# Attention keys re-partitioned through a DRAM scratch tensor instead of by ScalarE copies

## The chip, the cores and the metric

The kernel runs on one core of one Trainium2 chip. The metric is device time in microseconds (us) of one execution. The median of three runs is 1271.83 us (1271.44 to 1271.86). The core's engines are named as in the profile: PE is TensorE (PEld its weight loads), DVE is VectorE, ACT is ScalarE, POOL is GpSimd and SP is SyncE, which issues transfers and computes nothing.

## The reference

Two decoder layers are computed for one sequence of 256 positions and a width of 2048. Each layer projects the residual stream `x` with one wide matrix, feeds three mixers side by side (dilated sliding-window attention, a spatial gating unit, a chunked mLSTM), multiplies each by a SiLU gate, projects the result back and applies `x = LayerNorm(alpha * x + out)`.

The change touches the attention alone. It has three groups of eight heads of 64 columns, with windows and dilations (128, 1), (512, 4) and (2048, 16). Cut to what matters:

```
aq, ak = apply_partial_rope(aq, cos, sin), apply_partial_rope(ak, cos, sin)
for gi, (window, dilation) in enumerate(ATT_GROUPS):
    q, k, v = the 8 heads of this group          # (256, 8, 64) each
    s = einsum('qc,kc->qk', q, k) * 64 ** -0.5   # per head, and per residue of the position mod dilation
    s = where(0 <= distance <= window // dilation, s, -inf)
    p = exp(s - max(s)); l = sum(p); o = (p @ v) / l; lse = max(s) + log(l)
att = sum over the groups of softmax(lse over groups) * o
```

Everything is float32.

## The kernel before

**Projections.** All weight columns pass as blocks of 512 columns, and a block as eight chunks of 256 rows (512 KB). SP loads a chunk into one of four buffers `w_raw` (L324) as soon as VectorE has finished with that buffer. ScalarE rounds it to `w_hi` (L736), VectorE subtracts to get the rest, `w_lo` (L1060), and TensorE runs 12 matmuls of 512 columns for the chunk (L373: high by high, high by low, low by high, for two row tiles of `x` and two halves of the chunk). `w_hi` and `w_lo` have four buffers each, so ScalarE and VectorE can be four chunks ahead of TensorE and no more. The order of work on every engine is written out by hand; each engine runs its list in order and stops at each semaphore until it has the value asked for.

**A group of the attention.** It has four blocks, in this order: queries (block `n0`), keys (`n0 + 1`), values (`n0 + 2`) and an mLSTM gate (`n0 + 3`). The three groups run in the order dilation 4, dilation 16, dilation 1. The first two are the compressed groups (`g < NCOMP`): positions are kept by their residue mod 4, and only keys of the same residue are scored. The third uses bands of 128 by 128.

The keys come out of the projection with positions on the partitions, and the scores want head columns on the partitions. The way there is:

- ScalarE and VectorE copy the block's two halves from PSUM into `z` (`take`).
- GpSimd applies the rotary turn (`rope(1)`), six instructions.
- VectorE transposes in 32 by 32 squares into `zT[1]`, a part of `arena` (`turn(1)`, L1133 for the third group, two instructions of L1137 for the others). In its list that stands after the split of the last chunk of block `n0 + 2` and before the first of block `n0 + 3`.
- The squares lie on the wrong partitions then. ScalarE moves them with 16 copies of 32 partitions by 256 numbers (`moved(1, ...)`, L807 for the compressed groups, L810 for the third) from `zT[1]` to `kT`, eight after the split of chunk 0 of block `n0 + 3` and eight after that of chunk 1. The last one counts up `qkT_act`.
- TensorE waits for that count and runs the scores: `comp_scores` (64 matmuls, L546) after chunk 1 of block `n0 + 3` in the compressed groups, `scores(0)` and `scores(1)` (L506, L507) after chunk 0 of it in the third. Then come chunks of the same block again, and between them, in the third group, the transposes of the probabilities (L518).

Queries go the same way during block `n0 + 2`, with 16 copies of their own.

SP's list holds the loads in the order of the chunks, and a few loads of gate rows:

```
sp.wait_ge(w_lo_done, (l * NBLK + n) * CH + (c + 1))
sp.dma_start(w_raw[:, c % RING], ...).then_inc(w_landed[c % RING], 16)
```

The lines that matter:

Of the kernel before, what the change touches and what calls it, by code (L numbers as in the profile page):

```python
# [21 lines left out]
P = 128  # L22
DEPTH, SEQ, D = 2, 256, 2048
# [13 lines left out]
NCOMP = 2  # L37
RES = 4
LEN = SEQ // RES
# [50 lines left out]
def hybrid_layers(nc, x, x_t, positions, w_in, gate_w, w_out, gate_bias, sgu_g, sgu_b, w_spatial, b_spatial,  # L90
                  conv_w, conv_b, head_g, ln_g, ln_b, ln_b_t, out):
    with ExitStack() as ctx:
# [20 lines left out]
        kT = arena[:, 1024:2048].rearrange("p (m t) -> p m t", m=PAIRS)  # L113
# [5 lines left out]
        qTr, kTr = (m.rearrange("p m (r i) -> p m r i", r=RES) for m in (qT, kT))  # L119
# [61 lines left out]
        stat_dram = nc.dram_tensor("stat_dram", (DEPTH, SEQ, 2 * HEADS), F32, kind="Internal").ap()  # L181
        gmax_dram = nc.dram_tensor("gmax_dram", (DEPTH, MH, SEQ), F32, kind="Internal").ap()
# [36 lines left out]
        qk_ps, qkT_act, qkT_dve = sem("qk_ps"), sem("qkT_act"), sem("qkT_dve")  # L219
# [79 lines left out]
        def _(sp):  # L299
            for l in range(DEPTH):  # L300
                def load(w, n, col, order, gate=()):

                    for c in range(CH):
# [15 lines left out]
                        if l == 0 and n == 0:  # L319
# [7 lines left out]
                                     ).then_inc(w_landed[c % RING], 16)  # L327

# [22 lines left out]
        def _(pe):  # L351
# [5 lines left out]
            for l in range(DEPTH):  # L357
# [134 lines left out]
                for g in range(GROUPS):  # L492
# [4 lines left out]
                    def scores(p):  # L497

                        if p == 0:
                            pe.wait_ge(qkT_act, qk + 2)  # L500
                            pe.wait_ge(comp_og_act, comp)
                            pe.wait_ge(comp_og_dve, comp)
                        for h in range(2):
                            rows = slice(HD * h, HD * (h + 1))
                            o = ps[4 + 2 * (p % 2) + h]
                            pe.matmul(o[:, 0:P], qT[rows, p, 0:P], kT[rows, p, 0:P], start=True, stop=True)  # L506
                            mm = pe.matmul(o[:, P:3 * P], qT[rows, p, P:2 * P], kT[rows, p, :],  # L507
# [30 lines left out]
                    def comp_scores():  # L538

                        pe.wait_ge(qkT_act, qk + 2)  # L540
# [182 lines left out]
        def _(act):  # L723
# [5 lines left out]
            for l in range(DEPTH):  # L729
# [55 lines left out]
                for g in range(GROUPS):  # L785
# [12 lines left out]
                    def moved(which, first, last):  # L798

                        act.wait_ge(turned, qk + which + 1)  # L800
                        for i in range(first, last):
                            u, f = i // 4, i % 4
                            src = zT[which][u * 32:(u + 1) * 32]
                            dst = (qT, kT)[which][f * 32:(f + 1) * 32]
# [7 lines left out]
                        if last == 16:  # L812
                            mv_.then_inc(qkT_act, 1)
# [56 lines left out]
                    for i in range(4):  # L870
                        split(n0 + 2, i, i + 1)
                        moved(0, 4 * i, 4 * i + 4)
# [900 lines left out]
```

## Time and profile before

| what | value |
|---|---|
| median of three runs | 1271.83 us |
| span of the profiled execution, first to last instruction | 1269.9 us |
| PE busy | 1257.0 us (99%) |
| PEld busy | 1040.2 us (82%) |
| DVE busy | 893.0 us (70%) |
| ACT busy | 705.4 us (56%) |
| POOL busy | 244.0 us (19%) |
| mean granted clock of TensorE | 0.997 |
| moved by DMA | 264.97 MB, 209 GB/s over the span |

The profiled execution's own time is its span of 1269.9 us; the median of the timed runs is 1.9 us above it. Busy time of PE is the union of matmuls that overlap, so it tells that there was always one under way, not at which pace; the pace is read from the chain of waits, where a stretch of matmuls stands with its length and count. A wait shows as idle time in front of an instruction, with the engine and line that ended it. The view of one line of DMA issues gives the time from the issue to the landing of the last byte.

### The profile page before, as it was taken

Reading aid. Unit: us, or ns where it says so; the run is one execution under the profiler, and the core shown is the slowest. Engines: PE = TensorE matmul, PEld = TensorE weight load, DVE = VectorE, ACT = ScalarE, POOL = GpSimd, SP = SyncE. Lnnn points to the kernel's source line nnn. Section 1 sums busy time; section 2 is a strip of 40 time slices with the busy share of each in tenths; the row PEclk is TensorE's granted clock in tenths of the full one; section 3 lists DMA queues with packets and bytes.
Section 4 is the critical chain, followed back from the end, with each engine's and each line's share of the span. In section 5 each row is a group of like instructions: output and inputs, shape, how many; then the busy total and the mean of one; then the engine's idle time right before and its main releaser. Section 6 shows DMA issues by size and latency. Waiting matters only on the chain.

```text
span 1269.9 us, 16388 instructions
## 1 busy us (share of the span) xinstructions
PE 1257.0 (99%) x6342; PEld 1040.2 (82%) x6342; DVE 893.0 (70%) x1229; ACT 705.4 (56%) x989; POOL 244.0 (19%) x268
## 2 busy tenths in 40 slices
PE   9999999999999999999999999999999999999996
PEld 8888888878888888888888788888888888888885
DVE  5686876876667655865785779768665776567656
ACT  5477476575555544444563775666755555345441
POOL 0321522522220000400003223334131200004000
PEclk9999999999999999999999999999999999999998
DMA  9968768765665555465657587678546556565562
GB/s 336 310 209 261 236 189 277 260 192 164 204 195 174 184 186 185 152 230 190 207 186 238 183 282 245 193 258 282 184 149 215 183 157 209 165 197 198 186 212 86
DMA packets 129277, 264.97 MB, mean 209 GB/s; under 512 B 8824, under 2 KB 8976, under 8 KB 128688
## 3 DMA queue, kind: packets, MB, share of 16 engines
q1 hardware_dynamic: 123712, 247.23, 60.6%
q0 software_dynamic: 3680, 13.28, 3.0%
q10 hardware_dynamic: 1808, 3.42, 0.7%
q8 instruction: 50, 0.82, 0.3%
q14 instruction: 27, 0.22, 0.0%
HBM read 258.61 MB, written 5.28 MB: 208 GB/s over the span
## 4 chain that ended last, share of the span: by engine, by line
PE 86%; ACT 4%; DVE 4%; POOL 3%; issue 2%; DVEq 0%; POOLq 0%; ACTq 0%
PE ps L373 79%; ACT arena L810 2%; DVE w_lo L1060 2%; ACT w_hi L736 2%; PE ps L444 1%; PE ps L671 1%; PE ps L391 1%; PE ps L639 1%; POOL arena L1684 1%; PE ps L533 0%; POOL arena L1680 0%; PE ps L518 0%; ACT arena L807 0%; PE ps L355 0%; DVE arena L1133 0%
## 5 line engine op out<-in xcount | busy, mean ns | idle before, releaser
L1060 DVE TENSOR_TENSOR w_lo<-w_raw,w_hi 128x1024 fp32r<-128x1024 f32 x408 | 527.1, 1305 | 326.4 <-ACT w_hi L736 324.5
L736 ACT ACTIVATE w_hi<-w_raw 128x1024 fp32r<-128x1024 f32 x408 | 427.3, 1058 | 388.9 <-PE ps L373 339.3
L373 PE MATMUL ps<-w_hi,xT_hi 128*128 128x512 f32 x1616 | 636.2, 394 | 0.7 <-DVE w_lo L1060 0.7
L373 PE MATMUL ps<-w_hi,xT_lo 128*128 128x512 f32 x1616 | 629.6, 390 | 0.0
L373 PE MATMUL ps<-w_lo,xT_hi 128*128 128x512 f32 x1616 | 629.0, 389 | 0.0
L373 PEld LDWEIGHTS ps<-w_hi,xT_hi 128*128 128x128 f32 x1616 | 303.4, 188 | 64.3 <-issue 1.3
L373 PEld LDWEIGHTS ps<-w_hi,xT_lo 128*128 128x128 f32 x1616 | 303.3, 188 | 64.0
L373 PEld LDWEIGHTS ps<-w_lo,xT_hi 128*128 128x128 f32 x1616 | 303.6, 188 | 61.4
L292 POOL TENSOR_TENSOR carried<-ident 1x1 f32<-1x1 f32 x30 | 19.6, 652 | 454.8 <-DVE arena L1416 178.7
L1217 DVE CUSTOM_DVE_ANT_0 mix<-xres,mix 128x1024 f32<-128x1024 f32 x64 | 89.0, 1390 | 1.1
L807 ACT ACTIVATE arena<-arena 32x256 f32<-32x256 f32 x128 | 53.2, 416 | 15.6 <-DVE arena L1137 14.0
L373 PE MATMUL ps<-ahead,xT_hi 128*128 128x512 f32 x160 | 49.8, 392 | 0.0
L1630 POOL TENSOR_TENSOR su<-z,sincos 128x128 f32<-128x128 f32 x24 | 23.6, 1005 | 122.0 <-ACT z L796 100.9
L1404 DVE SCALAR_TENSOR_TENSOR conv_y<-ps,cw,conv_y 128x255 f32<-128x255 f32 (+2 forms) x96 | 41.7, 476 | 1.1
L1060 DVE TENSOR_TENSOR ahead<-w_raw,ahead 128x1024 fp32r<-128x1024 f32 x23 | 27.5, 1223 | 15.1 <-ACT ahead L736 15.0
L736 ACT ACTIVATE ahead<-w_raw 128x1024 fp32r<-128x1024 f32 x23 | 23.8, 1056 | 22.8 <-DMA w_raw<-w_out_dram 7.2
L373 PEld LDWEIGHTS ps<-ahead,xT_hi 128*128 128x128 f32 x160 | 29.7, 188 | 5.9
L373 PE MATMUL ps<-ahead,xT_lo 128*128 128x512 f32 x80 | 31.2, 390 | 0.0
L810 ACT ACTIVATE arena<-arena 32x256 f32<-32x256 f32 x64 | 26.6, 416 | 7.3 <-DVE arena L1133 6.5
L825 ACT ACTIVATE arena<-arena 32x256 f32<-32x256 f32 x64 | 26.6, 415 | 6.8 <-DVE arena L1165 5.9
L967 ACT ACTIVATE arena<-conv_y 128x512 f32<-128x512 f32 x16 | 10.1, 633 | 32.7 <-DVE conv_y L1404 32.7
L1732 POOL TENSOR_TENSOR store<-store,hg 128x1024 f32<-128x1024 f32 x4 | 11.4, 2876 | 76.5 <-DVE store L1462 76.5
(244 smaller groups left out, 825.3 us busy)
## 6 DMA issues: line engine op xcount, KB each, us to landing
w_raw<-w_in_dram SPq DMA_DIRECT2D x367, 512.0 KB, 4.5
w_raw<-w_out_dram SPq DMA_DIRECT2D x64, 512.0 KB, 4.8
mix<-gate_w_dram SPq DMA_DIRECT2D x32, 512.0 KB, 5.6
xres<-x_dram ACTq DMA_DIRECT2D x4, 512.0 KB, 8.4
v_dram<-arena POOLq DMA_DIRECT2D x4, 512.0 KB, 6.3
z<-v_dram POOLq DMA_DIRECT2D x8, 256.0 KB, 5.6
z<-ln_g_dram POOLq DMA_DIRECT2D x2, 1024.0 KB, 7.7
store<-ln_b_dram POOLq DMA_DIRECT2D x2, 1024.0 KB, 7.9
```

Source lines behind the costliest of these rows:

```text
L292: nc.gpsimd.tensor_tensor(carried[0:1, at:at + 1], ident[0:1, 0:1], ident[0:1, 0:1], ALU.mult)
L373: mm = pe.matmul(ps[2 * s + t][:], a[:, order[c] * KC + k, t * P:(t + 1) * P], b[:, k], start=(c + k + i == 0), stop=(c == CH - 1 and k == ...
L391: tr = pe.transpose(ps[4 + u % 4][:, (k * TT + t) * P:(k * TT + t + 1) * P], src[:, t, at * P:(at + 1) * P], ident[:])
L444: mm = pe.matmul(ps[t][:], a[:, c * KC + k, t * P:(t + 1) * P], b[:, k], start=False, stop=(c == CH - 1 and k == KC - 1 and i == 2))
L736: A(hi_of(n, c), w_raw[:, c % RING], ACT.Copy).then_inc(w_hi_done, 1)
L807: mv_ = A(dst.rearrange("p m (r t u i) -> p u t (m r) i", r=RES, t=TT, u=4)[:, u], src.rearrange("p (t f q i) -> p f t q i", t=TT, f=4, i= ...
L810: mv_ = A(dst.rearrange("p m (t u s) -> p u t m s", t=TT, u=4)[:, u], src.rearrange("p (t m f s) -> p f t m s", t=TT, m=PAIRS, f=4)[:, f], ...
L825: e = A(pTC[f * 32:(f + 1) * 32, :, u * 32:(u + 1) * 32], zp[u * 32:(u + 1) * 32].rearrange("p (s f i) -> p f s i", s=SLOTS, f=4)[:, f], A ...
L1060: TTn(lo_of(n, c), w_raw[:, c % RING], hi_of(n, c).bitcast(F32), ALU.subtract).then_inc(w_lo_done, 1)
L1217: f = V.tensor_tensor_reduce(gate_junk, xres[:, tt, half * KH:(half + 1) * KH], gate_rows[buf], 1.0, 0.0, ALU.mult, ALU.add, gate_acc[:, t ...
L1404: f = STT(y, ps[4 + hf][:, t * SEQ:(t + 1) * SEQ - back], cw[:, m, j:j + 1], y, ALU.mult, ALU.add)
L1630: G.tensor_tensor(rope_a[:, :, :, c], v[:, :, :, c], trig(1), ALU.mult)
```

## The change

For the keys, the sixteen ScalarE copies of a group are replaced by transfers that SP issues. A DRAM tensor `k_dram` of 128 by 1024 numbers per layer and group is added. `put_keys` waits for VectorE's transposes and stores `zT[1]` there: two transfers of 256 KB in the compressed groups, one of 512 KB in the third, in runs of 512 bytes. `fetch_keys` waits until the store has landed and loads `kT` back with four transfers of 128 KB, each for 32 partitions, again in runs of 512 bytes. They stand in SP's list after the load of chunk 3 and after the load of chunk 4 of block `n0 + 3`. TensorE waits for the four landings (`kT_landed`) where it waited for the copies.

The keys have another order inside a partition: blocks of 128 numbers, each with 32 positions of the four head pairs. The score matmuls read them as runs of 8 numbers (compressed groups) or 32 numbers (third group) with 128 numbers from run to run; before, a run was contiguous. In the third group VectorE writes its transposes in the order that the store needs, in runs of 32 numbers. The queries' copies stay, and so does the place of everything else; the splits of chunks 0 to 2 of block `n0 + 3` now follow one another on ScalarE.

```diff
+        kTr = kT.rearrange("p (b m r i) -> p m r b i", b=SEQ // QUARTER, m=PAIRS, r=RES)
+        kTt = kT.rearrange("p (b m s) -> p m b s", b=SEQ // QUARTER, m=PAIRS)
...
+        k_dram = nc.dram_tensor("k_dram", (DEPTH, GROUPS, 4, TT, 4, QUARTER, P), F32, kind="Internal").ap()
...
+                def put_keys(g):
+                    sp.wait_ge(turned, l * (GROUPS * 2) + g * 2 + 2)
+                    dst = k_dram[l, g].rearrange("f t u j x -> t (u j) f x")
+                    src = zT[1].rearrange("p (t f x) -> p t f x", t=TT, f=4)
+                    if g < NCOMP:
+                        for t in range(TT):
+                            sp.dma_start(dst[t], src[:, t]).then_inc(kT_put, 16)
+                    else:
+                        dst = k_dram[l, g].rearrange("f t u j x -> (u j) (f t) x")
+                        sp.dma_start(dst, zT[1].rearrange("p (a x) -> p a x", a=4 * TT)).then_inc(kT_put, 32)
+                def fetch_keys(g):
+                    sp.wait_ge(kT_put, (l * GROUPS + g + 1) * 32)
+                    src = k_dram[l, g].rearrange("f t u j x -> f j (t u) x")
+                    dst = kT.rearrange("p (b x) -> p b x", b=SEQ // QUARTER)
+                    for f in range(4):
+                        sp.dma_start(dst[f * QUARTER:(f + 1) * QUARTER], src[f]).then_inc(kT_landed, 16)
...
+                        if N_LOOP < n < N_SU and (n - N_LOOP) % 4 == 3:
+                            if c == 3:
+                                put_keys((n - N_LOOP) // 4)
+                            if c == 4:
+                                fetch_keys((n - N_LOOP) // 4)
...
-                            pe.wait_ge(qkT_act, qk + 2)
+                            pe.wait_ge(qT_act, l * GROUPS + g + 1)
+                            pe.wait_ge(kT_landed, (l * GROUPS + g + 1) * 4 * 16)
...
-                            pe.matmul(o[:, 0:P], qT[rows, p, 0:P], kT[rows, p, 0:P], start=True, stop=True)
-                            mm = pe.matmul(o[:, P:3 * P], qT[rows, p, P:2 * P], kT[rows, p, :],
+                            pe.matmul(o[:, 0:P], qT[rows, p, 0:P], kTt[rows, p, 0:P // QUARTER], start=True, stop=True)
+                            mm = pe.matmul(o[:, P:3 * P], qT[rows, p, P:2 * P], kTt[rows, p],
...
-                                                   kTr[rows, p, r, :], start=True, stop=True)
+                                                   kTr[rows, p, r], start=True, stop=True)
...
-                    split(n0 + 3, 0, 1)
-                    moved(1, 0, 8)
-                    split(n0 + 3, 1, 2)
-                    moved(1, 8, 16)
-                    split(n0 + 3, 2, 3)
+                    split(n0 + 3, 0, 3)
...
-                            V.transpose(zT[which], z[:, which].rearrange("p t c -> p (t c)")).then_inc(turned, 1)
+                            into = zT[which].rearrange("p (f b s) -> p b f s", f=4, b=TT * PAIRS) if which else zT[which]
+                            V.transpose(into, z[:, which].rearrange("p t c -> p (t c)")).then_inc(turned, 1)
```

## Rows read from the trace of the kernel before

**Rows 1.** The page, busy us of each engine (share of the span), count.

```profile
PE 1257.0 (99%) x6342; PEld 1040.2 (82%) x6342; DVE 893.0 (70%) x1229; ACT 705.4 (56%) x989; POOL 244.0 (19%) x268
```

**Rows 2.** The chain of waits in order of time: start us, us, what.

```profile
99.22 1.09 PE ps L546 x64
100.31 24.71 PE ps L373 x108
...
728.41 1.09 PE ps L546 x64
```

**Rows 3.** Waits of PE: line, waited for, us in total, times, longest.

```profile
PE ps L373 <- DVE w_lo L1060: 0.7, 1, 0.7
```

**Rows 4.** Timeline of PE, third groups: start us, us, instructions, [idle before <- releaser].

```profile
276.32 0.50 PE L506 MATMUL ps<-arena 64*128 64x128 f32 x4 [0.46 <-ACT arena L810]
...
905.01 0.50 PE L506 MATMUL ps<-arena 64*128 64x128 f32 x4
```

**Rows 5.** View of line L518: idle before it, us, times.

```profile
  ACT arena L839: 1.0, 2
```

**Rows 6.** The page, copy groups: count | busy us, mean ns | idle before.

```profile
L807 ACT ACTIVATE arena<-arena 32x256 f32<-32x256 f32 x128 | 53.2, 416 | 15.6 <-DVE arena L1137 14.0
...
L810 ACT ACTIVATE arena<-arena 32x256 f32<-32x256 f32 x64 | 26.6, 416 | 7.3 <-DVE arena L1133 6.5
```

**Rows 7.** Timeline of ACT, third group, layer 0: the last eight copies.

```profile
272.87 3.40 ACT L810 ACTIVATE arena<-arena 32x256 f32<-32x256 f32 x8
```

**Rows 8.** Timeline of DVE, the keys' transposes of four of the six groups.

```profile
86.53 2.09 DVE L1137 STREAM_TRANSPOSE arena<-z 128x512 f32<-128x512 f32 x2
...
267.10 1.23 DVE L1133 STREAM_TRANSPOSE arena<-z 128x1024 f32<-128x1024 f32 x1
...
716.90 2.09 DVE L1137 STREAM_TRANSPOSE arena<-z 128x512 f32<-128x512 f32 x2
...
895.78 1.23 DVE L1133 STREAM_TRANSPOSE arena<-z 128x1024 f32<-128x1024 f32 x1
```

**Rows 9.** View of line L324, five windows: issue ns, start; then issue to landing.

```profile
L324 SPq DMA_DIRECT2D w_raw<-w_in_dram x1: 367/367/367, 267.2 to 267.2; - x1
DMA to landing us min/median/max: 5.2/5.2/5.2
...
L324 SPq DMA_DIRECT2D w_raw<-w_in_dram x1: 368/368/368, 269.5 to 269.5; - x1
DMA to landing us min/median/max: 4.7/4.7/4.7
...
L324 SPq DMA_DIRECT2D w_raw<-w_in_dram x1: 368/368/368, 274.1 to 274.1; - x1
DMA to landing us min/median/max: 3.4/3.4/3.4
...
L324 SPq DMA_DIRECT2D w_raw<-w_in_dram x1: 368/368/368, 717.0 to 717.0; - x1
DMA to landing us min/median/max: 4.9/4.9/4.9
...
L324 SPq DMA_DIRECT2D w_raw<-w_in_dram x1: 368/368/368, 895.9 to 895.9; - x1
DMA to landing us min/median/max: 4.8/4.8/4.8
```

**Rows 10.** DMA issues by line: count, KB each, median us from issue to landing.

```profile
z<-v_dram POOLq DMA_DIRECT2D x8, 256.0 KB, 5.6
...
out_dram<-xres SPq DMA_DIRECT2D x4, 512.0 KB, 2.7
arena<-o_dram POOLq DMA_DIRECT2D x2, 512.0 KB, 4.6
```

**Rows 11.** Busy us by window: PE, PEld, DVE, ACT, POOL, granted clock, DMA.

```profile
1259.90:1262.70 2.80, 0.00 (x0) 0.00 (x0) 2.70 (x6) 0.29 (x1) 0.00 (x0) 1.00 0.00 0
1263.00:1269.90 6.90, 0.00 (x0) 0.00 (x0) 3.73 (x4) 0.00 (x0) 0.00 (x0) 0.50 0.38 152
```

More of the change, by code:

```diff
@@ L38 @@
 RES = 4
+QUARTER = P // 4
 LEN = SEQ // RES
@@ L112, in hybrid_layers @@
         qT = arena[:, 0:1024].rearrange("p (m t) -> p m t", m=PAIRS)
-        kT = arena[:, 1024:2048].rearrange("p (m t) -> p m t", m=PAIRS)
+        kT = arena[:, 1024:2048]
         vA = arena[:, 2048:3072].rearrange("p (t c) -> p t c", t=TT)
@@ L118, in hybrid_layers @@
         oacc = arena[:, 6400:7424].rearrange("p (t c) -> p t c", t=TT)
-        qTr, kTr = (m.rearrange("p m (r i) -> p m r i", r=RES) for m in (qT, kT))
+        qTr = qT.rearrange("p m (r i) -> p m r i", r=RES)
+        kTr = kT.rearrange("p (b m r i) -> p m r b i", b=SEQ // QUARTER, m=PAIRS, r=RES)
+        kTt = kT.rearrange("p (b m s) -> p m b s", b=SEQ // QUARTER, m=PAIRS)
         vS = vA.rearrange("p t (h q d) -> p t q h d", h=2, q=PAIRS)
@@ L218, in hybrid_layers @@
         mask_set, roped, turned = sem("mask_set"), sem("roped"), sem("turned")
-        qk_ps, qkT_act, qkT_dve = sem("qk_ps"), sem("qkT_act"), sem("qkT_dve")
+        qT_act, kT_put, kT_landed = sem("qT_act"), sem("kT_put"), sem("kT_landed")
         scored, masked, probs = sem("scored"), sem("masked"), sem("probs")
@@ L538, in comp_scores @@
                     def comp_scores():
-                        pe.wait_ge(qkT_act, qk + 2)
+                        pe.wait_ge(qT_act, l * GROUPS + g + 1)
+                        pe.wait_ge(kT_landed, (l * GROUPS + g + 1) * 4 * 16)
                         for j in range(TT):
@@ L796, in take, with moved @@
                         A(dst, src, ACT.Copy).then_inc(z_act, 1)
-                    def moved(which, first, last):
-                        act.wait_ge(turned, qk + which + 1)
+                    def moved(first, last):
+                        act.wait_ge(turned, qk + 1)
                         for i in range(first, last):
                             u, f = i // 4, i % 4
-                            src = zT[which][u * 32:(u + 1) * 32]
-                            dst = (qT, kT)[which][f * 32:(f + 1) * 32]
+                            src = zT[0][u * 32:(u + 1) * 32]
+                            dst = qT[f * 32:(f + 1) * 32]
                             if g < NCOMP:
@@ L812, in moved @@
                         if last == 16:
-                            mv_.then_inc(qkT_act, 1)
+                            mv_.then_inc(qT_act, 1)
                     def comp_exponentials():
@@ L871, in _ @@
                         split(n0 + 2, i, i + 1)
-                        moved(0, 4 * i, 4 * i + 4)
+                        moved(4 * i, 4 * i + 4)
                     take(n0 + 2, 0, z[:, 1, 0, :])
                     split(n0 + 2, 4, 8)
-                    split(n0 + 3, 0, 1)
-                    moved(1, 0, 8)
-                    split(n0 + 3, 1, 2)
-                    moved(1, 8, 16)
-                    split(n0 + 3, 2, 3)
+                    split(n0 + 3, 0, 3)
                     if g < NCOMP:
```

## The prediction

> **What bounds the kernel now.** The first view to read is the page's list of busy times. TensorE (PE) is busy for 1257.0 of the 1269.9 us of the span [rows 1]; ScalarE (ACT), from which the copies go, is busy for 56% of it. The second is the chain of waits, in order of time: long pieces of it are the projection matmuls and nothing else, and one shows their pace: 108 matmuls, nine weight chunks of 12, in 24.71 us, so 2.75 us a chunk [rows 2]. The third is what TensorE waited for. The view of its waits has one delay of a matmul by VectorE (DVE) over the whole program, 0.7 us [rows 3]; the score matmuls of the third group wait 0.46 us for ACT's key copies in layer 0 and for nothing that the row shows in layer 1 [rows 4]; the transposes of the probabilities have 1.0 us of idle weight loading before them, for the exponentials [rows 5]. Together that is 2.2 us; the first of them is in the query part of a group, which the change leaves alone. What the change can give back is therefore at most 0.5 + 1.0 us, while a key matrix that comes late stops TensorE at once, since its instructions run in order.
>
> **What is removed.** Half of the 128 copies of L807 and half of the 64 of L810, 416 ns each [rows 6]: 96 copies, 40 us of ACT time over the program, 6.7 us a group. None of that is on TensorE's path by itself. In the stretch before the scores of the third group, layer 0, the last eight copies run from 272.87 to 276.27 [rows 7], and the two weight splits that were put between them came in time for TensorE. So the 40 us are worth nothing but the waits named above: 0.5 us for the scores of layer 0, and some of the 1.0 us before the probabilities, because ACT and VectorE reach them with no backlog of splits. Of that last one I take 0.4 (between 0 and 1.0; part of an idle weight load lies beside matmuls still draining). The query copies stay, and VectorE's order of work stays.
>
> **What is added, and where it waits.** The keys' way after VectorE's transposes is now: SyncE (SP) sees the semaphore, one or two transfers of 512 KB in all to DRAM, their landing, four transfers of 128 KB back, their landing, the scores. The distance that this has to fit in is from the end of the transposes to the start of the scores. For the third group: 267.10 + 1.23 = 268.33 to 276.32, and 895.78 + 1.23 = 897.01 to 905.01 [rows 4, 8], so 8.0 us in both layers, of which 7.5 in layer 0 before TensorE is idle. For the other two groups, whose scores come one chunk later: 86.53 + 2.09 = 88.62 to 99.22 is 10.6 us [rows 2, 8], two more groups show the same within 0.1, and layer 1's first has only 718.99 to 728.41, 9.4 us [rows 2, 8].
>
> *The store.* It enters SP's queue right behind weight loads that are still in flight. In layer 0's third group the load issued at 267.2 lands after 5.2 us, at 272.4, and the next one in the queue, issued at 269.5, lands after 4.7, at 274.2, which is 1.8 us later [rows 9]. The store is issued at 268.4 and takes that place, so I let it land 1.8 us after the load in front of it. Its rows are 512 bytes long, and no row shows such a store; the bounds are 0 and 1.0 us more: a 512 KB load of 2 KB rows from POOL takes 4.6 us where half as much in 1 KB rows takes 5.6 [rows 10]. I take 0.4, nearer to the load in the same queue. The store lands at 274.6. An alone store of 512 KB takes 2.7 us [rows 10], which is the low end: 271.1.
>
> *The fetch.* SP is woken, and issues four transfers at 0.37 us each. A load with nothing in front of it takes 3.4 us [rows 9]; that is the low end, counted from the first issue. Counted from the last it is 3.4 + 1.1 = 4.5, and behind another load 4.7 [rows 9]. The data of the first three moves while the fourth is issued, so I take 3.4 + 0.7, and again 0.4 for the short rows: 4.5 us.
>
> *Sum by group.* Layer 0, third: 274.6 + 4.5 = 279.1 against 276.32, so 2.8 us later. Layer 1, third: the load issued at 895.9 lands after 4.8, at 900.7 [rows 9]; plus 1.8, 0.4 and 4.5 is 907.4 against 905.01, 2.4 us later. Layer 1, first: the load at 717.0 lands after 4.9, at 721.9 [rows 9]; plus 6.7 is 728.6 against 728.41, 0.2 us. The other three have 1.2 us more room than that one and stay hidden with about 1 us to spare. Together 2.8 + 2.4 + 0.2 - 0.4 = **5.0 us slower**. So 0.9 us of waits go, and larger ones stand in the same places.
>
> *Edits that I cost at nothing.* SP's wait for the store holds the loads of chunks 5 to 7 of that block behind it: chunk 5 was issued at 274.1 in layer 0 [rows 9] and now goes after the fetch's issues, at about 276. It lands some 4 us after that, while TensorE needs it four chunks of 2.75 us after the scores; without that cover every us of SP's wait over 5 would be lost. The transfers add 1 MB a group to the queues, as much as two weight chunks of the 32; their queueing is already in the 1.8 us, and the loads behind them have the same four chunks of room. In the third group VectorE writes its transposed keys in runs of 32 instead of in one piece: between 1.23 us (contiguous) and 2.09 us (the two strided ones of the other groups) [rows 8]. The store waits for the loads in front of it for longer than that, so it costs nothing. The score matmuls read keys in runs of 8 or 32 numbers that are 512 bytes apart; no row shows a moving operand like that. Between 0 and a doubling of 1.09 us [rows 2] in four groups, I take 0, the value of the row that stands for as many matmuls of as many columns.
>
> **The rivals.**
>
> 1. *The transfers run as if alone and the keys are in time* (not slower). Store 2.7 and fetch 3.4 make 6.1 us after the transposes: 274.4 and 903.1, before TensorE comes to the scores. It decides from 7.5 us of both together. For it: the store is SBUF to DRAM, and one such is the fastest large transfer of the profile. Against: loads are in flight at the moment of issue in each of the six groups. Gain 0.5 + 0.4, so 1270.9. The Trainium skill, page DMA: Bandwidth & Descriptors, section Anatomy of one DMA — SWDGE (gpsimd) path, gives a transfer about 2.0 us plus its bytes over 436 GB/s; by that an estimate is 3.2 us for 512 KB and 6.4 for the two, and the sum would end here. The trace agrees for a load alone (3.4 us) and not for loads behind others (4.7 to 5.2) [rows 9].
>
> 2. *TensorE's clock falls in the new wait.* After the last matmul the granted clock is still 1.00 over 2.8 us without TensorE work, and 0.50 in the stretch from 1263 on [rows 11]. My wait in layer 0 is 279.1 - 275.9 = 3.2 us. If the clock falls to 1.2 GHz, each chunk until it rises costs 2.75 us more; one or two chunks make 2.7 to 5.5, and with one of the two waits over the edge the time is about 1281. Against: the waits are at the edge of what that row shows, and the matmuls around them are dense. The Trainium skill, page TensorE: Matmul & The Clock Gate, section HAM oscillation — how this bites in real kernels, says that waits for transfers can send the array back to half rate so that the next work starts slow; rows 11 show the fall, and no row of this case shows the price.
>
> 3. *Short rows and four small transfers cost 1 us more in each direction.* Then the third groups lose 4.8 and 4.4, layer 1's first 2.2, and each of the other three 1.0: 14.4 - 0.4 = 14.0, so 1286. For it: the 1 KB rows of rows 10. Against: those are POOL's.
>
> 4. *The scores read the spread keys at half speed*: 4.4 us more, 1281.
>
> **How the numbers follow.** The profiled execution lasts 1269.9 us from first to last instruction, 1.9 below the median of 1271.83, and 5.0 us are added to both: 1274.9 and **1276.8 us**. What a measurement of this kernel can tell from no change is about 0.2%, 2.5 us. Chances: the forecast 0.52, its own range 1273.5 to 1279.5; rival 1 0.15; rival 2 0.16; rival 3 0.13; rival 4 0.04. No case reaches a gain of 2.5 us, since the three waits together are 2.2: faster 0.02, for what the trace does not show. Same takes rival 1 and the low tenth of the forecast, 0.23; the rest is slower, 0.75. The range is from rival 1, 1271, to rival 3, 1286, which leaves out the far side of rivals 2 and 3.
>
> **What would show it.** Right: a TensorE gap of 2 to 4 us before the scores of the third group in both layers, released by the fetch; none or under 1 us in the other groups; a store that lands about 6 us after the transposes, a fetch 4 to 5 us after its first issue; ACT about 40 us less busy at an unchanged pace of 2.75 us a chunk. Wrong: scores of the third group that start within 0.5 us of where they did; gaps of several us in all six groups; a granted clock under 1.00 behind a gap; or a pace that changes away from the scores, which would say that ACT's copies cost TensorE something that no wait shows.

## The result and the profile after

The changed kernel takes 1280.13 us, the median of four runs (1276.17 to 1280.63), where the kernel before takes 1271.82 beside it: a ratio of 1.006, with a 95% interval of 1.0045 to 1.0074. That is 8.3 us slower, 3.3 more than the sum of the prediction. The profiled execution took 1279.92 us, with a span of 1278.2.

The page's busy times of the changed kernel, to be read against [rows 1]:

```profile
PE 1258.5 (98%) x6342; PEld 1041.7 (81%) x6342; DVE 895.8 (70%) x1229; ACT 667.9 (52%) x893; POOL 242.5 (19%) x268
```

ScalarE is relieved of 96 instructions and 37.5 us; TensorE runs the same 6342 matmuls in 1.5 us more. The rest of the loss is idle time of TensorE. The view of PE's waits in the changed kernel (line, waited for: us in total, times, longest), against [rows 3]:

```profile
PE ps L536 <- issue: 5.8, 2, 3.4
PE ps L577 <- DMA arena<-k_dram: 1.6, 1, 1.6
PE ps L384 <- POOL ident L1595: 1.6, 1, 1.6
PE ps L402 <- DVE w_lo L1087: 0.7, 1, 0.7
```

The first two rows are new, and both stand in front of score matmuls: L536 in the third groups, L577 in a compressed one. The last two stand in the view of before as well, with the same 1.6 and 0.7 us. "Issue" names no releaser, but the timeline of PE gives the moment, and the queue's own timeline shows what landed then. PE's timeline of the changed kernel, three places, against [rows 4] and the second chain row of [rows 2]:

```profile
279.55 0.50 PE L536 MATMUL ps<-arena 64*128 64x128 f32 x4 [3.38 <-issue]
...
734.52 1.16 PE L577 MATMUL ps<-arena 64*64 64x64 f32 x64 [1.61 <-DMA arena<-k_dram]
...
913.62 0.50 PE L536 MATMUL ps<-arena 64*128 64x128 f32 x4 [2.38 <-issue]
```

SyncE's timeline of the changed kernel, the third group of layer 0, layer 1's first group and layer 1's third (L312 and L315 are the store, L323 the fetch, L348 weight loads):

```profile
267.36 0.37 SPq L348 DMA_DIRECT2D w_raw<-w_in_dram  x1
268.51 0.44 SPq L315 DMA_DIRECT2D k_dram<-arena  x1
269.62 0.38 SPq L348 DMA_DIRECT2D w_raw<-w_in_dram  x1
274.85 1.81 SPq L323 DMA_DIRECT2D arena<-k_dram  x4
...
723.56 0.92 SPq L312 DMA_DIRECT2D k_dram<-arena  x2
...
728.34 1.82 SPq L323 DMA_DIRECT2D arena<-k_dram  x4
...
903.23 0.39 SPq L315 DMA_DIRECT2D k_dram<-arena  x1
...
909.17 1.81 SPq L323 DMA_DIRECT2D arena<-k_dram  x4
```

The fetch's first issue is the moment at which SyncE saw the store landed. So the store took 6.3 us in layer 0's third group (268.51 to 274.85) and 5.9 in layer 1's, and the last of the four fetches landed 4.6 and 4.4 us after the first issue, 0.1 us ahead of the scores. Keys that were done at 268.5 are usable at 279.5.

The starts of the same 6342 matmuls in the two traces give where the 8.3 us came in (us, later than before):

| place | change |
|---|---|
| the first 10 us of the program | +0.27 |
| third group's scores, layer 0 | +2.92 |
| the matmuls behind them, at half clock | +1.46 |
| probabilities' transposes, layer 0 | -0.23 |
| first group's scores, layer 1 | +1.69 |
| third group's scores, layer 1 | +2.43 |
| probabilities' transposes, layer 1 | -0.21 |
| sum | 8.3 |

The first line is not the change's: in the traces of the other kernels below, the same matmuls come between 0.3 us earlier and 0.7 us later than before. The third line is read from the busy times by window, whose last three figures are the granted clock, the DMA engines' share and GB/s:

```profile
275.70:279.60 3.90, 0.52 (x5) 0.13 (x3) 0.60 (x1) 1.06 (x1) 0.00 (x0) 1.00 0.89 235
280.40:283.80 3.40, 3.40 (x15) 2.36 (x13) 3.21 (x21) 1.79 (x8) 0.00 (x0) 0.50 0.69 259
283.80:290.00 6.20, 6.20 (x32) 5.15 (x31) 2.46 (x3) 3.72 (x12) 0.00 (x0) 1.00 0.40 108
```

After 3.4 us without a matmul the granted clock is still 1.00 when the scores start at 279.55; it is 0.50 from 280.4 to 283.8, and full again after. The DMA engines are 89% busy during the wait: weight loads and key transfers at once.

The line in the table for layer 1's first group has a cause of its own. Its fetch took 6.0 us, from 728.34 to 734.38; the chain of waits of the changed kernel shows the last of its four pieces, which took 4.7, where the median of all 24 is 2.6:

```profile
729.69 4.69 DMA arena<-k_dram
```

What ran beside it is GpSimd's store of the group's values, 512 KB. Its row in GpSimd's timeline of the changed kernel, then of the one before:

```profile
728.80 0.78 POOL L1677 DMA_DIRECT2D v_dram<-arena  x1 [0.28 <-issue]
```

```profile
730.99 0.78 POOL L1649 DMA_DIRECT2D v_dram<-arena  x1
```

TensorE's matmuls stand 4.4 us later there than before (the first four lines of the table), so against them the values' store came 6.6 us earlier: 0.5 us behind the fetch's first issue, where before it came behind the scores. The timelines of ScalarE and VectorE show why. ScalarE's half of the values, which the store waits for, stood behind two times eight key copies; VectorE's half, taken at 729.18, stood behind a split that waited 3.28 us for ScalarE, which these copies held up. Both halves are now taken at 727.50. ScalarE and VectorE before, then ScalarE in the changed kernel:

```profile
723.53 3.40 ACT L807 ACTIVATE arena<-arena 32x256 f32<-32x256 f32 x8
726.95 1.06 ACT L736 ACTIVATE w_hi<-w_raw 128x1024 fp32r<-128x1024 f32 x1
727.91 0.58 ACT L796 ACTIVATE arena<-ps 128x512 f32<-128x512 f32 x1
```

```profile
728.04 1.22 DVE L1060 TENSOR_TENSOR w_lo<-w_raw,w_hi 128x1024 fp32r<-128x1024 f32 x1 [3.28 <-ACT w_hi L736]
```

```profile
727.50 0.60 ACT L827 ACTIVATE arena<-ps 128x512 f32<-128x512 f32 x1 [1.31 <-PE ps L402]
```

### The profile page after: what moved, and what is told of

Same layout as the page of the kernel before. It is cut to its first block, busy times and chain, and to the rows that moved or that the text cites. A ratio compares the mean times of both kernels' runs of the same rounds, so it can differ in the third digit from the quotient of the medians.

```text
span 1278.2 us, 16332 instructions
## 1 busy us (share of the span) xinstructions
PE 1258.5 (98%) x6342; PEld 1041.7 (81%) x6342; DVE 895.8 (70%) x1229; ACT 667.9 (52%) x893; POOL 242.5 (19%) x268
## 4 chain that ended last, share of the span: by engine, by line
PE 95%; DVE 1%; issue 1%; ACT 1%; DMA 1%; SPq 0%; DVEq 0%; POOL 0%; POOLq 0%; ACTq 0%
PE ps L402 88%; PE ps L473 1%; PE ps L702 1%; PE ps L420 1%; PE ps L670 1%; DVE w_lo L1087 1%; PE ps L563 0%; ACT arena L838 0%; PE ps L548 0%; PE ps L384 0%; DMA arena<-k_dram 0%; PE ps L577 0%; PE ps L596 0%; DMA k_dram<-arena 0%; ACT w_hi L767 0%
## 5 line engine op out<-in xcount | busy, mean ns | idle before, releaser
L296 POOL TENSOR_TENSOR carried<-ident 1x1 f32<-1x1 f32 x30 | 13.7, 458 | 435.4 <-DVE arena L1444 178.7
L856 ACT ACTIVATE arena<-arena 32x256 f32<-32x256 f32 x64 | 26.6, 415 | 6.8 <-DVE arena L1193 6.0
L838 ACT ACTIVATE arena<-arena 32x256 f32<-32x256 f32 x64 | 26.6, 416 | 5.5 <-DVE arena L1165 4.6
```

The costliest lines, as they stand in the source:

```text
L296: nc.gpsimd.tensor_tensor(carried[0:1, at:at + 1], ident[0:1, 0:1], ident[0:1, 0:1], ALU.mult)
L838: mv_ = A(dst.rearrange("p m (r t u i) -> p u t (m r) i", r=RES, t=TT, u=4)[:, u], src.rearrange("p (t f q i) -> p f t q i", t=TT, f=4, i= ...
L856: e = A(pTC[f * 32:(f + 1) * 32, :, u * 32:(u + 1) * 32], zp[u * 32:(u + 1) * 32].rearrange("p (s f i) -> p f s i", s=SLOTS, f=4)[:, f], A ...
```

## The experiments

Theory T: the loss is the scores' wait for the keys' way through DRAM; that way is long because weight loads, and in one group the store of the values, run on the same DMA engines (or meet in the DRAM behind them, which no run here tells apart); and the clock falls behind the longest wait. Rivals: A, the transfers slow the rest of the kernel, whoever waits for them. B, the form of the transfers (512-byte runs, four pieces) makes them slow. C, the store is late only because of its place in SyncE's queue. All ratios are to the kernel before on the same chip, with 95% intervals.

**1. Nobody waits for the keys.** All transfers run, but the fetch goes to a tile that nobody reads, and the scores read zeros, so the attention's values are not the reference's. Later steps that write over the store's source wait for the store instead (not shown).

```
+        kT_aside = sb("kT_aside", [P, 1024])
-                    dst = kT.rearrange("p (b x) -> p b x", b=SEQ // QUARTER)
+                    dst = kT_aside[:].rearrange("p (b x) -> p b x", b=SEQ // QUARTER)
-                            pe.wait_ge(kT_landed, (l * GROUPS + g + 1) * 4 * 16)
+                G.memset(kT, 0.0)
```

> All transfers run, at the places they have in the changed kernel, but the fetch lands in a tile of its own and the scores read zeros in place of the keys (left out: the scores' use of the keys); so no matmul waits for a transfer. Theory (the time is lost where the scores wait for the fetch, and by the clock behind such a wait): the three waits of 2.9, 1.7 and 2.4 us and the 1.5 us at half clock go, so about 8.5 us off the changed kernel: 1271 to 1272, no granted clock under 1.00 after the first 10 us. Rival A (the added traffic, SP held at the store, or the reads of keys in short runs cost it): 1276 or more, with gaps or a slower pace elsewhere.

1270.84 us, ratio 0.9992 (0.9983 to 1.0001). PE's waits in it:

```profile
PE ps L388 <- POOL ident L1602: 1.6, 1, 1.6
PE ps L406 <- DVE w_lo L1092: 0.7, 1, 0.7
PE ps L461 <- ACT ahead L797: 0.4, 1, 0.4
```

No score waits, the granted clock stays up, and the whole loss is gone. The transfers themselves cost nothing that can be measured: A is out. The medians are 0.9 us under the kernel before, with an interval that reaches no change; the starts of the same matmuls show where such a gain sits, 0.5 us at the third group's scores in layer 0 and 0.2 us at the probabilities' transposes of each layer. So ScalarE's 96 copies were worth about 0.9 us, and no arrangement that was tried gives more.

**2. The third group's keys by ScalarE again**, the compressed groups' as changed.

```
-                        if N_LOOP < n < N_SU and (n - N_LOOP) % 4 == 3:
+                        if N_LOOP < n < N_LOOP + NCOMP * 4 and (n - N_LOOP) % 4 == 3:
+                        moved_keys(0, 8)
                         split(n0 + 3, 1, 2)
+                        moved_keys(8, 16)
```

> The compressed groups' keys go by transfers, the third group's by ScalarE copies in the old order. Theory: the losses of the third groups go (2.9 + 2.4 us and 1.5 us at half clock), the 0.4 us before the probabilities come back, and the 1.7 us of layer 1's first group stay: 1273 to 1274. Rival A (traffic and short runs, spread evenly over six groups): two thirds of the 8.3 us stay, about 1277. Rival B (the wait in layer 1's first group is an accident of one execution): 1271.5 to 1272.5.

1272.78 us, ratio 1.0009 (1.0000 to 1.0018), a little under the forecast. The row of its PE waits for the keys:

```profile
PE ps L579 <- DMA arena<-k_dram: 0.7, 1, 0.7
```

Layer 1's first group still waits, and the third groups lose next to nothing: their scores start 0.15 us sooner in layer 0 and 0.25 us later in layer 1 than before. So 7.3 of the 8.3 us hang on the third groups' transfers and on what they bring (less of a wait in layer 1's first group is among it: 0.8 us there instead of 1.7; why that one shrank was not tried by itself).

**3. TensorE kept at work in the wait**: ten matmuls of the identity ahead of the third group's wait, into a bank that is free there.

```
+                            for _ in range(10):
+                                pe.matmul(ps[7][:, 0:P], ident[:], ident[:], start=True, stop=True)
                             pe.wait_ge(qT_act, l * GROUPS + g + 1)
                             pe.wait_ge(kT_landed, (l * GROUPS + g + 1) * 4 * 16)
```

> Ten matmuls of the identity by itself, which nobody reads, stand before TensorE's wait for the third group's keys; they take about 2.3 us of it. Theory (the clock fell because TensorE was idle): the granted clock stays 1.00 behind layer 0's third group, and 1.5 us go where the clock fell: 1276 to 1278.7, with the scores no later than they were. Rival C (the clock falls for another reason, or the fill delays the scores): 1280 or more.

1277.57 us, ratio 1.0046 (1.0032 to 1.0059): 2.6 us less than the changed kernel. PE's timeline around the wait, and the busy times of the window there:

```profile
276.42 2.39 PE L532 MATMUL ps<-ident 128*128 128x128 f32 x20
279.07 0.50 PE L538 MATMUL ps<-arena 64*128 64x128 f32 x4 [0.26 <-DMA arena<-k_dram]
```

```profile
278.30:281.00 2.70, 2.44 (x23) 1.87 (x21) 0.96 (x8) 0.00 (x0) 0.00 (x0) 1.00 0.99 362
```

The scores still come late, by 2.0 us in layer 0 and 2.7 in layer 1, but the clock stays at 1.00, there and in the 5 us behind it, and its mean is 0.997 or 0.998 in all five runs. With something to wait on, the view names the releaser too: the fetch. So the fall of the clock belongs to a TensorE that stands idle and is paid on top of the wait, 1.46 us in the profiled execution of the changed kernel. The rest of the 2.6 us is not the clock's: the wait in layer 0 was itself 0.9 us shorter (the store took 5.8 us, not 6.3), and layer 1's first group lost 1.1 us, not 1.7; why was not tried. The changed kernel's four timed runs spread over 4.5 us, and the shortest is the one with the highest mean clock (0.997, the others 0.994 to 0.996), which fits a fall that comes in some runs and not in others; but the kernel of this experiment spreads over 2.7 us too, so the fall is not all of it.

**4. The store ahead of one load**: in all six groups, the store goes in front of the load of chunk 3 and not behind it.

```
+                        if N_LOOP < n < N_SU and (n - N_LOOP) % 4 == 3 and c == 3:
+                            put_keys((n - N_LOOP) // 4)
                         sp.wait_ge(w_lo_done, (l * NBLK + n) * CH + (c + 1))
...
-                            if c == 3:
-                                put_keys((n - N_LOOP) // 4)
```

> The store stands in SP's list ahead of the load of chunk 3 and no longer behind it, so one load less is in front of it in the queue. Theory (the store's 6.3 us in the third group are mostly the loads in front): it lands about 1.6 us earlier in the third groups and 1 to 1.5 in the others, the scores follow, and the clock does not fall: 1273.5 to 1276. Rival D (a store to DRAM of 512-byte runs takes its 5 to 6 us whatever stands in front): within 1 us of the changed kernel, 1279 to 1281.

1282.62 us, ratio 1.0081 (1.0067 to 1.0095): a miss, slower even than the changed kernel. SyncE's timeline, third group of layer 0:

```profile
271.00 0.44 SPq L315 DMA_DIRECT2D k_dram<-arena  x1
271.48 1.50 SPq L350 DMA_DIRECT2D w_raw<-w_in_dram  x2
275.32 1.81 SPq L323 DMA_DIRECT2D arena<-k_dram  x4
```

The store did get quicker, 4.3 us instead of 6.3. But the two loads issued right behind it were now in front of the fetch, which took 6.6 us instead of 4.6 (the last one landed at 281.94): 10.9 us in both kernels from the store's issue to the keys. What one leg gains the other gives back, as long as the loads go between them. What makes this kernel slower than the changed one is the compressed groups, of which three wait for the keys here and one there:

```profile
PE ps L577 <- DMA arena<-k_dram: 3.1, 3, 1.6
```

**5. The values' store waits for the keys**:

```
                         carry_pool()
+                        pool.wait_ge(kT_landed, (l * GROUPS + g + 1) * 4 * 16)
                         pool.dma_start(v_dram[l, g].rearrange("(t p) c -> p t c", p=P), vA).then_inc(v_stored, 16)
```

> GpSimd's store of the values (512 KB), which in the changed kernel comes during the keys' fetch because ScalarE is done with its list earlier, waits for the keys' landing. Theory (in layer 1's first group the fetch took 6.0 us instead of 4.7 because that store ran beside it): the fetch takes 4.5 to 4.8 us in all compressed groups and the wait of 1.7 us there falls under 0.5; the third groups are as in the changed kernel; 1.2 to 1.5 us less in the sum of the waits. Rival F (the fetch varies by itself): a wait of 1 us or more in some compressed group.

1275.90 us, ratio 1.0040 (1.0028 to 1.0052), 4.2 us less than the changed kernel. The one row that PE's waits have left for scores:

```profile
PE ps L536 <- issue: 4.6, 2, 3.0
```

The row of L577 is gone, and the fetch of that group takes 4.8 us instead of 6.0 (727.45 to 732.27): the collision with the values' store is shown. It is not the scatter of one trace: numbers 9 to 12 below hold that store back too and lose at most 0.1 us there, while numbers 2, 3 and 6, whose compressed groups are the changed kernel's, lose 0.8, 1.1 and 1.2. The third groups, which have no such store, still wait. The medians differ by more than the 1.7 us of this group: in the profiled execution (1277.16 us) the third groups lose 2.5 and 1.7 us, 0.4 and 0.7 less than in the changed kernel, and the clock falls as it does there; why they lose less was not tried.

**6. Another form of transfer** in the third group: four stores with runs of 1 KB, one fetch with runs of 4 KB.

```
+                        for u in range(4):
+                            sp.dma_start(k3_dram[l, :, :, u, :].rearrange("f j x -> j f x"), src[u * QUARTER:(u + 1) * QUARTER]).then_inc(kT_put, 16)
...
+                        sp.dma_start(kT, k3_dram[l].rearrange("f j u x -> (f j) (u x)")).then_inc(kT_landed, 64)
```

> Third group only: the store goes as four transfers of 128 KB in runs of 1 KB, the fetch as one of 512 KB in runs of 4 KB. Theory (the loads in the queue set when the store lands; the fetch is 3.4 us of a lone load and 1.3 us of three further issues): the store lands where it did within 0.5 us, the fetch takes 3.4 to 3.8 us instead of 4.6, the waits of the third groups are 1 us shorter and the clock does not fall: about 1276.5. Rival G (the fetch waits for the load in front of it whatever its form): fetch 4.4 us or more, 1278 to 1281.

1277.55 us, ratio 1.0043 (1.0027 to 1.0058), its profiled execution 1280.66. SyncE's timeline, layer 0:

```profile
268.00 1.99 SPq L317 DMA_DIRECT2D k_dram<-arena  x4
...
273.40 0.42 SPq L323 DMA_DIRECT2D arena<-k_dram  x1
273.86 11.37 SPq L353 DMA_DIRECT2D w_raw<-w_in_dram  x4
```

One fetch with runs eight times as long took 5.7 us (273.40 to 279.06), longer than the four short ones, probably because the next loads were issued 0.5 us behind it and not 1.9; that was not tried by itself. The third groups lost 3.1 and 2.8 us, and the clock was at 0.50 for 6.8 us of the profiled execution, which cost another 2.8. So another form does not help beside the loads; that the short runs cost little in themselves is shown by numbers 11 and 12, where a store in 512-byte runs takes 3.2 us with no load near, against 2.7 for the large store of [rows 10]. B is out as the cause.

**7. Store and fetch ahead of the loads of chunks 3 and 4, in all six groups.**

```
+                        if N_LOOP < n < N_SU and (n - N_LOOP) % 4 == 3 and c == 3:
+                            put_keys((n - N_LOOP) // 4)
+                            fetch_keys((n - N_LOOP) // 4)
+                        weights(c)
```

> Store and fetch both stand ahead of the loads of chunks 3 and 4, so neither has a fresh load in front of it. Theory (each 512 KB load that stands in the queue before the store or between store and fetch costs the keys about 2 us, wherever it stands): store 4.2 us, fetch 4.0 to 4.6, the keys land 8.2 to 8.8 us after the transposes instead of 11.0; waits of at most 1 us in the third groups and none in the others, no fall of the clock: 1271.3 to 1273. Rival E (chunks 3 and 4 are then late for TensorE): gaps of 1 to 3 us in front of the projection matmuls two or three chunks after the scores, 1274 or more.

1274.53 us, ratio 1.0022 (1.0014 to 1.0031). SyncE's timeline in the third group of layer 0, then the first row of PE's waits:

```profile
267.98 0.44 SPq L315 DMA_DIRECT2D k_dram<-arena  x1
271.83 1.81 SPq L323 DMA_DIRECT2D arena<-k_dram  x4
273.69 2.81 SPq L331 DMA_DIRECT2D w_raw<-w_in_dram  x4
```

```profile
PE ps L404 <- DVE w_lo L1089: 2.6, 2, 1.9
```

With no load between the two legs, the keys are there 8.0 us after the store's issue, no score waits, and the clock stays up. The price moved: in layer 1's first group four loads come in a bunch from 724.33 on, behind the fetch and beside the values' store, take 5.2 to 9.7 us, and a projection chunk waits 1.9 us for its weights.

**8. Another queue**: ScalarE issues the store and the fetch, SyncE only loads.

```
+                    split(n0 + 3, 0, 1)
+                    put_keys(g)
+                    split(n0 + 3, 1, 2)
+                    fetch_keys(g)
+                    split(n0 + 3, 2, 3)
```

> Store and fetch are issued by ScalarE, on its own queue, and SP's list has only the loads. Theory (it is the order in SP's queue): the transfers pass the loads, store 3.5 us and fetch 4.0 to 4.6 us, keys 7.5 to 8.5 us after the transposes, waits of the third groups under 1 us: 1271.3 to 1273. Rival H (the 16 engines are shared, and the transfers lose as much to the loads beside them as they lost behind them): keys still 10 us or more after the transposes, 1277 or more. Rival I (ScalarE, held at the store's landing, is late with its splits): gaps in front of the projection matmuls.

1282.76 us, ratio 1.0088 (1.0075 to 1.0101). ScalarE's timeline, third group of layer 0:

```profile
268.25 0.64 ACTq L746 DMA_DIRECT2D k_dram<-arena  x1
...
275.51 1.85 ACTq L754 DMA_DIRECT2D arena<-k_dram  x4
```

On a queue with no load in it the store took 7.3 us, longer than anywhere: C is out. SyncE, which no longer waited for it, put one more load beside it. The scores waited 3.5 and 2.8 us, and the clock fell behind both waits. The Trainium skill, page DMA: Bandwidth & Descriptors, section Issuing engines are not separate DMA queues, says that transfers from any issuing engine run on the same 16 DMA engines and interleave; these 7.3 us agree.

**9 and 10. The best parts together**: in the third group store and fetch ahead of the loads of chunks 3 and 4, the compressed groups as changed, the values' store behind the keys. Number 9 also has the third group's transposes one weight split earlier.

```
+                        if n == N_SU - 1 and c == 3:
+                            put_keys(NCOMP)
+                            fetch_keys(NCOMP)
...
+                        pool.wait_ge(kT_landed, (l * GROUPS + g + 1) * 4 * 16)
... number 9 only:
-                    split(n0 + 2, 6, 8)
+                    split(n0 + 2, 6, 7 if g == NCOMP else 8)
                     turn(1)
+                    if g == NCOMP:
+                        split(n0 + 2, 7, 8)
```

> Third group: store and fetch ahead of the loads of chunks 3 and 4, and VectorE's key transposes before its split of chunk 7 of the values' block instead of behind it (1.2 us earlier); compressed groups as in the changed kernel, with GpSimd's store of the values behind the keys' landing. Theory: keys land 8 us after the transposes and 1 us before the scores in the third groups, no wait there, and none over 0.4 us in the compressed groups, no fall of the clock: 1270.8 to 1271.8, at or under the kernel before by up to 1 us. Rival E (the loads of chunks 3 and 4 of the third group come late for TensorE or for the exponentials): gaps there of 0.5 us or more, 1272 to 1274.

> The same without the earlier transposes. Theory: the third groups' scores come within 0.3 us of the kernel before, as they did with both transfers ahead of the loads in all groups, and the late chunks of layer 1's first group (2.4 us there) are gone: 1271.3 to 1272.5, 0.5 to 1 us above the one with earlier transposes. Rival: 1273.5 or more, if the lateness came from holding the loads in the third group too.

Number 10: 1272.16 us, ratio 1.0004 (0.9995 to 1.0014), as expected. Number 9: 1273.62, ratio 1.0015 (1.0007 to 1.0024), a miss: earlier keys made it slower. SyncE's timeline of number 9, then of number 10, third group of layer 0:

```profile
265.11 1.76 SPq L351 DMA_DIRECT2D w_raw<-w_in_dram  x2
267.66 0.44 SPq L315 DMA_DIRECT2D k_dram<-arena  x1
273.40 1.95 SPq L323 DMA_DIRECT2D arena<-k_dram  x4
```

```profile
264.60 1.76 SPq L351 DMA_DIRECT2D w_raw<-w_in_dram  x2
268.29 0.44 SPq L315 DMA_DIRECT2D k_dram<-arena  x1
272.14 1.81 SPq L323 DMA_DIRECT2D arena<-k_dram  x4
```

The store of number 9 was issued 0.6 us earlier and landed 1.3 us later. The second of the two loads in the first row went out at 266.51 there, 1.15 us ahead of the store; in number 10 at 266.00, 2.29 us ahead.

**11 and 12. Is it the distance to the load in front?** Numbers 10 and 9 again, with the load of chunk 2 behind the fetch as well.

```
-                        if n == N_SU - 1 and c == 3:
+                        if n == N_SU - 1 and c == 2:
```

> As the kernel that sends the third group's store and fetch ahead of the loads of chunks 3 and 4 (and holds the values' store back until the keys have landed), but with the load of chunk 2 behind them too, so that the nearest load in front of the store was issued some 3.6 us before it, not 2.3. Theory (what counts is how far the load in front is from being done when the store is issued: 1.15 us after its issue the store took 5.5 to 6.4 us, 2.29 us after it 3.7 to 4.3): the store now takes 2.7 to 3.5 us, the fetch about 4.2, the keys are there 7 to 7.8 us after the transposes, no score waits, 1271.0 to 1272.2 us. Rival (the store has its own fixed time of about 3.8 us here, from its 512-byte rows): store 3.8, keys at 8.1 us as before. A risk for both: chunk 2 lands late and the projection waits 0.5 to 1.5 us instead.

> The same with the transposes of the third group one weight split earlier, as in the kernel that lost 1.9 us by that step. Theory (that loss was the store running into the load issued 1.15 us before it): with that load behind the fetch, the store, 2.5 us or more after the nearest load, takes 2.7 to 4 us instead of 5.7 to 6.0, the scores of the third group wait for nothing, 1271.0 to 1272.3 us. Rival (the earlier place of the transposes costs in itself, by VectorE's order of splits): the store still takes over 5 us or the projection waits for its splits, and the time stays at 1273 to 1274.

Number 12 (early transposes): 1272.01 us, ratio 1.0003 (0.9994 to 1.0012). Number 11: 1274.74, ratio 1.0027 (1.0018 to 1.0036). SyncE's timeline of number 12, third group of layer 0:

```profile
264.03 0.37 SPq L351 DMA_DIRECT2D w_raw<-w_in_dram  x1
266.58 0.44 SPq L315 DMA_DIRECT2D k_dram<-arena  x1
269.78 1.81 SPq L323 DMA_DIRECT2D arena<-k_dram  x4
```

The store takes 3.2 us there, and 3.2 in number 11. All third groups that use the transfers, layer 0 and layer 1 (us; the first column is the time from the last load's issue to the store's, the second from the store's issue to the fetch's first):

| kernel | behind the load in front | the store took |
|---|---|---|
| changed | 1.15, 1.16 | 6.3, 5.9 |
| 1 | 1.16, 1.16 | 6.4, 5.9 |
| 3 | 1.16, 1.15 | 5.8, 5.7 |
| 5 | 1.16, 1.15 | 5.7, 5.5 |
| 9 | 1.15, 1.16 | 5.7, 6.0 |
| 6 (four pieces, 1 KB runs) | 1.15, 1.15 | 5.4, 5.3 |
| 8 (ScalarE's queue) | 1.16, 1.16 | 7.3, 6.6 |
| 4 | 2.29, 2.29 | 4.3, 4.3 |
| 7 | 2.29, 2.29 | 3.9, 3.7 |
| 10 | 2.29, 2.29 | 3.9, 4.0 |
| 12 | 2.55, 2.56 | 3.2, 3.2 |
| 11 | 3.70, 3.69 | 3.2, 3.2 |

So the theory of the store holds in both: the earlier transposes of number 9 cost nothing in themselves, and the same transposes with the load out of the way are 1.6 us faster. On the time, number 11 is a miss, and the risk named with it came true in another place. Its PE waits have this row at their head, which [rows 3] don't have:

```profile
PE ps L551 <- ACT arena L873: 3.3, 2, 1.7
```

The load of chunk 2 landed so late that ScalarE stood 8 us without a weight to split, and in VectorE's order the masking and maxima of the scores come behind two splits that then came late: they began at 281.27, 5.6 us after the scores, and the exponentials and the transposes behind them were late by as much as the row shows. In number 12 the loads went out 1.3 us sooner, and they begin at 279.96. No version beats the kernel before; numbers 10 and 12 equal it.

## Why the prediction was right and where it was not

**The mechanism was right, and the size short by two terms.** The 1280.13 us are above the forecast's own 1273.5 to 1279.5 and near the 1281 of rival 2, but less than half of what was missed is that rival's. ScalarE's copies were off TensorE's path, and the keys' way through DRAM put them on it: experiment 1 takes the wait alone away, and the loss goes with it. Its 1270.84 is also what rival 1 gave for keys that are in time, 1270.9, so the 0.9 us that the copies were worth was sized right as far as the noise lets one see, and the probabilities' share of it (forecast 0.4) measured 0.44 in the changed kernel's trace.

**The third groups' terms** measured +2.92 and +2.43, forecast 2.8 and 2.4. The first of them is right by two errors that cancel. The load in front was forecast to land at 272.4; it took 6.0 us, to 273.3, because the store ran into it. The store landed 1.5 us after it, not 2.2, at 274.8 (forecast 274.6). And the picture behind it, a place in SyncE's queue, was wrong: experiment 8 shows the same and worse from another queue. What counts, by experiments 4 and 7 to 12, is which loads are in flight before the store and between store and fetch. The fetch, forecast 4.5 us, took 4.6 and 4.4.

**The term that failed is layer 1's first group: forecast +0.2, measured +1.69.** The step said that the store and fetch need 6.7 us beyond the load in front; it did not ask what a freer ScalarE would start earlier. The values' store of GpSimd came 6.6 us sooner against the matmuls and ran beside the fetch; experiment 5 removes that, and the wait is gone. The other three groups stayed hidden, as forecast.

**Rival 2 came true beside the forecast, not in place of it.** The clock did fall behind the wait of layer 0, which the prediction had named as a sign of being wrong. The Trainium skill, page TensorE: Matmul & The Clock Gate, section HAM oscillation — how this bites in real kernels, says that such waits send the array back to half rate, so that the next work starts cold; the 3.4 us at 0.50 agree with the fall, and the first 0.85 us of scores at 1.00 do not agree with the cold start. The price was put at 2.7 to 5.5 us and measured 1.46, since the clock was down for 3.4 us, and not for one or two whole chunks; in number 6, where it was down for 6.8 us, it was 2.8. In layer 1 a wait of 2.4 us left it up. Sum of what was missed: 1.5 for the first group of layer 1, 1.46 for the clock, 0.27 at the start of the program, which is scatter, nearly all of the 3.3.

**Rivals 3 and 4.** Longer runs in fewer transfers did not help (experiment 6), and a store in rows of 512 bytes took 3.2 us with no load near (numbers 11 and 12), so it was not the rows. The strided keys cost TensorE nothing: the matmuls that read them, in the changed kernel and before it (ns, min, median, max; the higher maximum is the half clock):

```profile
L536 PE MATMUL ps<-arena x32: 269/272/470, 279.6 to 930.2; 64*128 64x128 f32 x32
```

```profile
L506 PE MATMUL ps<-arena x32: 269/272/373, 276.3 to 921.9; 64*128 64x128 f32 x32
```

VectorE's transposes in runs of 32 took 1.23 us, as before. The chance of "same" does not add up: 0.15 and a tenth of 0.52 make 0.20, not 0.23.

**The cover that was named held, but had an end.** SyncE's waits cost the weights nothing in the changed kernel, whose one wait for a split is still 0.7 us. Where the loads were put behind the keys to help them, that cover ran out: one wait of 1.9 us in experiment 7, two of together 3.3 in number 11.

## What to carry to other kernels

Taking work off an engine that is not the bound is worth only the waits that it ends (here about 0.9 us of 40), so compare the new path's length with the slack at its consumer, and read that path's transfers under the load of the stretch, not from a transfer that ran alone. Ask what the relieved engine will start earlier, and on what shared resource that lands. If a store and its fetch must go through DRAM in a stream of loads, leave room between the load in front and the store (some 2.5 us between their issues, for the 512 KB of this case) and put no load between store and fetch, but only as far as the loads behind them can wait.

## What the runs showed of the hardware

How long a 512 KB store takes behind a 512 KB load depends on how long before it the load was issued: 5.5 to 7.3 us at 1.15 us, 3.7 to 4.3 at 2.29, 3.2 at 2.55 and at 3.70. Issued earlier into a fresh load it landed later in absolute time (number 9), and it slowed the load too (5.3 us against 4.6). The Trainium skill's figure of 2.0 us plus the bytes over 436 GB/s, page DMA: Bandwidth & Descriptors, section Anatomy of one DMA — SWDGE (gpsimd) path, is a fit for transfers that GpSimd issues, and gives 3.2 us as an estimate; SyncE's store agrees with it when no load is near, and is about twice as long when one is.

In the changed kernel the granted clock fell 0.85 us after matmuls had begun again, so the wait before it and the slow stretch behind it do not touch; a reader who looks only at the first scores after that wait will find them at full speed. It is not always so: in numbers 4, 5 and 8 the fall came 0.25 to 1.25 us behind the first score, in number 6 0.5 us ahead of it. Nor did the length of the wait alone decide: the clock fell behind 2.8 us (number 8, layer 1) and stayed up behind 3.0 (number 4, layer 1).
